# Where the second modulation is applied, and where the first expert's weights lie

## What is computed

```python
def trunk_layer(x, mods, p, ctx_kv_c, ctx_k_rope):
    shift1, scale1, gate1, shift2, scale2, gate2 = mods
    mix, c_kv, k_rope = token_mixer(x * (1 + scale1) + shift1, p, ctx_kv_c, ctx_k_rope)
    x = layer_norm(ALPHA * x + gate1 * mix, p['ln1_g'], p['ln1_b'])
    ffn = expert_choice_ffn(x * (1 + scale2) + shift2, p)
    x = layer_norm(ALPHA * x + gate2 * ffn, p['ln2_g'], p['ln2_b'])
    return x, c_kv, k_rope

def expert_choice_ffn(h, p):
    ...
    aff = jax.nn.softmax((tok @ p['w_router']).astype(jnp.float32), axis=-1)
    gate, idx = lax.top_k(aff.T, cap)
    xe = tok[idx]
    hid = jax.nn.silu(jnp.einsum('ecd,edf->ecf', xe, p['w_gate'])) * jnp.einsum('ecd,edf->ecf', xe, p['w_up'])
    ye = jnp.einsum('ecf,efd->ecd', hid, p['w_down']) * gate[..., None].astype(tok.dtype)
    ...
```

## Time and profile before

| What | Value |
|---|---|
| Time of three executions | 2191.76 us median (2188.12 to 2195.24) |
| Profiled execution | 2196.62 us, span 2194.8 us |
| PE busy | 2067.1 us, 94% of the span |
| DVE, ACT, POOL busy | 985.7, 181.4, 103.2 us |
| Read from memory | 649.44 MB, mean 299 GB/s |
| Mean granted TensorE clock | 0.981 |
| Chain that ended last | PE 73%, DMA 18%, DVE 6% |
| Expert gate and up matmuls (L1228) | 2048, 469.9 us busy, 43.6 us idle before them, of it 30.6 for w_gate loads |

### The profile page before, as it was taken

One profiled execution on the slowest core, in us unless ns is written; L12 is line 12 of the kernel. 1 busy time (PEld: TensorE's weight loads), 2 busy tenths in 40 slices (PEclk: granted clock), 3 DMA queues, 4 the chain that ended last, 5 costly groups with the idle time before them and its releaser, 6 DMA issues.

```text
span 2194.8 us, 21927 instructions
## 1 busy us (share of the span) xinstructions
PE 2067.1 (94%) x9470; PEld 1217.4 (55%) x9470; DVE 985.7 (45%) x1289; ACT 181.4 (8%) x418; POOL 103.2 (5%) x156
## 2 busy tenths in 40 slices
PE   6999999999999999999998999999999999989886
PEld 3455455555799999998874533333333333322222
DVE  4221365729799898997565221121112212121114
ACT  2111310000011111111010000000000000000000
POOL 1010010002110000100000000000000000000001
PEclk8999999999999999999999899999999999999998
DMA  9993036603376666667669699999999999999992
GB/s 344 402 347 115 0 114 218 229 20 106 113 242 233 220 231 232 228 230 282 238 245 368 247 405 435 431 430 430 430 432 431 432 429 426 431 433 430 430 429 115
DMA packets 138426, 657.39 MB, mean 300 GB/s; under 512 B 7137, under 2 KB 83643, under 8 KB 114201
## 3 DMA queue, kind: packets, MB, share of 16 engines
q1 hardware_dynamic: 125538, 586.05, 66.8%
q0 software_dynamic: 12304, 69.86, 8.8%
q10 hardware_dynamic: 488, 0.08, 0.0%
HBM read 649.44 MB, written 6.52 MB: 299 GB/s over the span
## 4 chain that ended last, share of the span: by engine, by line
PE 73%; DMA 18%; DVE 6%; SPq 1%; issue 1%; ACT 0%; DVEq 0%; ACTq 0%
DMA ring<-in_w_up_dram 13%; PE ps L1228 12%; PE ps L927 12%; PE ps L1262 8%; PE ps L1428 8%; PE ps L933 6%; PE ps L993 4%; DMA ring<-in_w_gate_dram 4%; PE ps L864 2%; PE ps L1045 2%; PE ps L736 2%; PE ps L1153 1%; PE ps L701 1%; PE ps L748 1%; PE ps L1170 1%; PE ps L1154 1%
## 5 line engine op out<-in xcount | busy, mean ns | idle before, releaser
L1228 PE MATMUL ps<-ring,arena 128*64 128x512 f32 (+1 forms) x2048 | 469.9, 604 | 43.6 <-DMA ring<-in_w_gate_dram 30.6
L1228 PEld LDWEIGHTS ps<-ring,arena 128*64 128x64 f32 (+1 forms) x2048 | 145.2, 138 | 355.6 <-issue 289.2
L2440 DVE TENSOR_TENSOR arena<-ps,arena 128x512 f32<-128x512 f32 x180 | 116.0, 686 | 398.5 <-PE ps L1170 398.5
L1262 PE MATMUL ps<-ring,arena 128*64 128x512 f32 x1024 | 224.6, 594 | 6.9 <-DMA ring<-in_w_down_dram 5.6
L1784 DVE SCALAR_TENSOR_TENSOR arena<-ring,arena 128x2048 f32<-128x2048 f32 x90 | 211.4, 2349 | 2.1
L927 PE MATMUL ps<-arena,ring 128*128 128x192 f32 x1024 | 174.4, 326 | 0.1
L927 PEld LDWEIGHTS ps<-arena,ring 128*128 128x128 f32 x1024 | 167.6, 190 | 1.5 <-issue 1.2
L1428 PE MATMUL ps<-arena,ring 128*128 128x384 f32 x512 | 165.6, 486 | 0.0
L1262 PEld LDWEIGHTS ps<-ring,arena 128*64 128x64 f32 x1024 | 71.5, 137 | 147.8 <-issue 135.9
L1428 PEld LDWEIGHTS ps<-arena,ring 128*128 128x128 f32 x512 | 97.2, 190 | 68.2 <-issue 0.9
L927 PE MATMUL ps<-ring 128*128 128x192 f32 x768 | 132.7, 326 | 0.0
(11 more groups left out here) (361 smaller groups left out, 1819.3 us busy)
## 6 DMA issues: line engine op xcount, KB each, us to landing
ring<-in_w_gate_dram SPq DMA_DIRECT2D x30, 4096.0 KB, 20.4
ring<-in_w_up_dram SPq DMA_DIRECT2D x30, 4096.0 KB, 21.8
ring<-in_w_down_dram SPq DMA_DIRECT2D x28, 4096.0 KB, 20.7
ring<-in_w_in_dram SPq DMA_DIRECT2D x29, 2048.0 KB, 8.6
ring<-in_w_ada_dram POOLq DMA_DIRECT2D x48, 1024.0 KB, 5.2
ring<-in_w_ada_dram SPq DMA_DIRECT2D x32, 1024.0 KB, 18.0
ring<-in_w_out_dram SPq DMA_DIRECT2D x16, 2048.0 KB, 11.5
ring<-in_w_ada_dram SPq DMA_DIRECT2D x8, 2048.0 KB, 12.9
```

The source lines that it names most:

```text
L1228: mm = pe.matmul(ps[j // 4][64 * half:64 * half + m, :], xe_w[g % 2][:, c0:c0 + m], w[:, k4, half * 512:(half + 1) * 512], start=(k == 0), ...
L1262: mm = pe.matmul(ps[3 + u % 2][64 * half:64 * half + 64, :], hidT[:, k % 4, 64 * (k // 4):64 * (k // 4) + 64], w[:, k2, u * 512:(u + 1) * ...
L2440: dve.tensor_tensor(out, ps[SCATTER_BANKS[q % 5]][:, :], out, ALU.add).then_inc(S["cb_used"], 1)
```

## The change

- h2 holds only the normalised rows: `modulated` becomes `normalised`, one instruction per half instead of two. Scale and shift are applied where D lies on the partitions: in the copies of the transposed tiles (for the router) and in the copies of the gathered rows (for the experts), with one number per partition (`col_r`, `col_e`) as pointer operands. Each copy of 512 or 384 columns becomes four instructions, one per block and, for the gathered rows, per group of tokens.
- The spread rows `mod_s` and `mod_c` go. POOL loads `col_e` and `mod_blocks` in eight small loads instead; PE transposes `mod_blocks` once, in latent unit 1, and DVE copies it to `col_r`.
- Blocks 6 and 7 of expert 0 (the last two up blocks) get memory of their own, `early`, in Y + 4096 and A_HT, and are issued ahead of all other expert blocks. The later blocks' places move up by two: (n - 2) % 6. The two regions of xe change places, and give and ye move.
- ln1 is loaded when PE has released block 6, and all three residuals stand together in expert 0, ahead of ye.
- Three semaphores of the front are merged into one (`ld_front`); these hunks are left out below, as are the lists of names.

```diff
@@ -78,9 +78,10 @@
     N_X0 = stream.index(("x0", 0, 0))
+    EARLY = (N_EXP + 6, N_EXP + 7)
...
                 (n - N_GATE) % 2 * 2 if n < N_OUT else OUT_PLACES[n - N_OUT] if n < N_EXP else
-                (n - N_EXP) % RING for n in range(N_ALL)]
+                n - N_EXP if n < EARLY[0] else None if n in EARLY else (n - N_EXP - 2) % RING for n in range(N_ALL)]
@@ -115,7 +116,6 @@
         x1T = view(A_MG + 3072, 2, NT)
-        mod_c = view(A_HT, 2, D)
@@ -131,6 +131,9 @@
         tri = view(o + 256, P)
+        col_r = view(o + 128, 2, 2, KD)
+        col_e = view(o + 192, 2, 2, KD)
+        mod_blocks = view(o + 418, P, parts=64)
@@ -249,7 +252,6 @@
         gate1 = view(Y, 2, D)
-        mod_s = view(Y + 4096, 2, D)
@@ -260,11 +262,12 @@
         XE = KD * GRP * 48
-        xe_off = (A_HT, Y)
+        early = [view(Y + 4096, SLOT), view(A_HT, SLOT)]
+        xe_off = (Y, A_HT)
...
         xe_w = [view(off, XE) for off in xe_off]
-        give = view(A_HT + XE, 3, GRP, P)
-        ye = view(A_HT + XE + 1536, 2, 512)
+        give = view(A_HT + 4096, 3, GRP, P)
+        ye = view(A_HT + XE, 2, 512)
...
@@ -313,11 +316,13 @@
         for n in range(N_ALL):
+            if n in EARLY:
+                continue
...
         def slot(n, *dims):
-            ap = ring[:, place_of[n], 0:math.prod(dims)]
+            ap = early[n - EARLY[0]] if n in EARLY else ring[:, place_of[n], 0:math.prod(dims)]
@@ -377,7 +382,10 @@
-            eng.wait_ge(used[place_of[n]], turn_of[n] + 1)
+            if n in EARLY:
+                eng.wait_ge(S["early_used"], n - EARLY[0] + 1)
+            else:
+                eng.wait_ge(used[place_of[n]], turn_of[n] + 1)
...
@@ -479,9 +487,16 @@
+            sp.wait_ge(S["ada_rows"], 6)
+            sp.dma_start(slot(EARLY[0], 4, FF), w_up_v[:, 0, 8:12, :]).then_inc(ld_early, 16)
+            sp.wait_ge(S["wo_done"], 16)
+            sp.dma_start(slot(EARLY[1], 4, FF), w_up_v[:, 0, 12:KD, :]).then_inc(ld_early, 16)
+
...
                     n = N_EXP + 12 * e + j
+                    if n in EARLY:
+                        continue
@@ -646,21 +661,21 @@
             pool.dma_start(w_router[:, :, 0:NE], t["w_router"][0].rearrange("(k p) n -> p k n", p=P)).then_inc(ld_wr, 16)
-            pool.wait_ge(S["wo_done"], 3)
-            for j in range(2):
-                pool.dma_start(mod_s[:, j, :], row(mods_dram[1 + j, 1], P)).then_inc(ld_mods, 16)
+            for kind in range(2):
+                for j in range(2):
+                    r0 = 32 * kind + 16 * j
+                    pool.dma_start(mod_blocks[r0:r0 + 16], mods_dram[1 + j, kind].rearrange("(k p) -> k p", p=P))\
+                        .then_inc(ld_mods, 16)
+                    pool.dma_start(col_e[:, kind, j, :], mods_dram[1 + j, kind].rearrange("(p k) -> p k", k=KD))\
+                        .then_inc(ld_mods, 16)
...
             pool.dma_start(gate1[:, 0, :], row(mods_dram[0, 0], P)).then_inc(ld_x2b, 16)
-            pool.wait_ge(S["wo_done"], 16)
-            for j in range(2):
-                pool.dma_start(mod_c[:, j, :], row(mods_dram[1 + j, 0], P)).then_inc(ld_modc, 16)
-            pool.wait_ge(S["h2_done"], 4)
+            pool.wait_ge(S["route_ps"], 5)
+            pool.memset(give.rearrange("p a b c -> p (a b c)"), 0.0).then_inc(gp, 1)
+            through(pool, EARLY[0])
...
             pool.dma_start(ln1[:, 1, :], row(t["ln1_b"][0], P)).then_inc(ld_ln1, 16)
-
-            pool.wait_ge(S["route_ps"], 5)
-            pool.memset(give.rearrange("p a b c -> p (a b c)"), 0.0).then_inc(gp, 1)
@@ -684,10 +699,13 @@
                     n -= (n - N_EXP) % 2
-                pe.wait_ge(full[place_of[n]], filled[n])
+                if n in EARLY:
+                    pe.wait_ge(ld_early, 32)
+                else:
+                    pe.wait_ge(full[place_of[n]], filled[n])
...
             def release(mm, n):
-                mm.then_inc(used[place_of[n]], 1)
+                mm.then_inc(S["early_used"] if n in EARLY else used[place_of[n]], 1)
@@ -1008,6 +1026,9 @@
                 out_product(r1, rows_11, w_11, True).then_inc(S["prod_ps"], 1)
+                if cb == 1:
+                    pe.wait_ge(ld_mods, 128)
+                    pe.transpose(ps[6][:, 0:64], mod_blocks, ident[0:64, 0:64]).then_inc(S["col_ps"], 1)
...
@@ -1665,8 +1686,12 @@
                         act.wait_ge(S["route_ps"], 2 * p - 1)
-                    act.activation(h2T[:, 4 * q:4 * q + 4, :].rearrange("p a b -> p (a b)"), ps[2 + q][:, :], ACT.Copy)\
-                       .then_inc(S["h2T_a"], 1)
+                    for b in range(4):
+                        kb = 4 * q + b
+                        ins = act.activation(h2T[:, kb, :], ps[2 + q][:, b * P:(b + 1) * P], ACT.Identity,
+                                             bias=col_r[:, min(TILES[p], 1), 0, kb:kb + 1],
+                                             scale=col_r[:, min(TILES[p], 1), 1, kb:kb + 1])
+                    ins.then_inc(S["h2T_a"], 1)
@@ -1684,6 +1709,7 @@
             table(ACT.Exp)
+            act.wait_ge(S["col_done"], 3)
@@ -1697,16 +1723,23 @@
                 act.wait_ge(S["xe_ps"], 8 * g + i + 1)
-                act.activation(xe[g % 2][:, 2 * i:2 * i + 2, :].rearrange("p a b -> p (a b)"), ps[bank][:, 0:384],
-                               ACT.Copy).then_inc(S["xe_a"], 1)
-
-            act.wait_ge(S["h2_done"], 6)
+                for k in (2 * i, 2 * i + 1):
+                    src = ps[bank][:, k % 2 * 192:k % 2 * 192 + 192].rearrange("p (a b) -> p a b", b=48)
+                    dst = xe[g % 2][:, k, :].rearrange("p (a b) -> p a b", b=48)
+                    for kind, cs in ((1, slice(0, CAP_S)), (0, slice(CAP_S, 48))):
+                        ins = act.activation(dst[:, :, cs], src[:, :, cs], ACT.Identity, bias=col_e[:, kind, 0, k:k + 1],
+                                             scale=col_e[:, kind, 1, k:k + 1])
+                ins.then_inc(S["xe_a"], 1)
+
+            act.wait_ge(ld_mods, 128)
+            act.wait_ge(S["wo_done"], 20)
...
                                          ps[half][:, kk * 128:(kk + 1) * 128].rearrange("p (a b) -> p a b", b=CAP_S),
-                                         ACT.Copy)
+                                         ACT.Identity, bias=col_e[:, 1, 0, 4 * half + kk:4 * half + kk + 1],
+                                         scale=col_e[:, 1, 1, 4 * half + kk:4 * half + kk + 1])
@@ -2279,17 +2312,13 @@
-            def modulated(p):
+            def normalised(p):
...
                 tile = TILES[p]
-                mods, ready = (mod_c, ld_modc) if tile == 0 else (mod_s, ld_mods)
-                dve.wait_ge(ready, 32)
...
                     cs = slice(half * 1024, (half + 1) * 1024)
-                    link(dve.scalar_tensor_tensor(h2[:, tile, cs], acc[:, tile, cs], lnv[:, tile, 0:1], mods[:, 1, cs],
-                                                  ALU.subtract, ALU.mult))
-                    dve.scalar_tensor_tensor(h2[:, tile, cs], h2[:, tile, cs], lnv[:, tile, 3:4], mods[:, 0, cs],
-                                             ALU.mult, ALU.add).then_inc(S["h2_done"], 1)
+                    dve.tensor_scalar(h2[:, tile, cs], acc[:, tile, cs], lnv[:, tile, 0:1], lnv[:, tile, 3:4],
+                                      ALU.subtract, ALU.mult).then_inc(S["h2_done"], 1)
@@ -2311,8 +2340,12 @@
                         dve.wait_ge(S["route_ps"], 2 * p - 1)
-                    dve.tensor_copy(h2T[:, 4 * q:4 * q + 4, :].rearrange("p a b -> p (a b)"), ps[2 + q][:, :])\
-                       .then_inc(S["h2T_d"], 1)
+                    for b in range(4):
+                        kb = 4 * q + b
+                        ins = dve.tensor_scalar(h2T[:, kb, :], ps[2 + q][:, b * P:(b + 1) * P],
+                                                col_r[:, min(TILES[p], 1), 1, kb:kb + 1],
+                                                col_r[:, min(TILES[p], 1), 0, kb:kb + 1], ALU.mult, ALU.add)
+                    ins.then_inc(S["h2T_d"], 1)
@@ -2370,31 +2403,33 @@
                     out_mix(cb + 1, 3)
+                if cb == 1:
+                    dve.wait_ge(S["col_ps"], 3)
+                    link(dve.tensor_copy(col_r.rearrange("p c m k -> p (c m k)"), ps[6][:, 0:64]))
+                    dve.sem_inc(S["col_done"], 1)
             spread(1, 1)
-            modulated(0)
+            normalised(0)
...
             h2T_copies(0)
-            modulated(1)
+            normalised(1)
...
             context_rows(1)
-            residual(0)
...
             context_rows(2)
-            residual(1)
...
             spread(0, 3)
-            modulated(2)
+            normalised(2)
@@ -2429,8 +2464,13 @@
                 dve.wait_ge(S["xe_ps"], 8 * g + i + 1)
-                dve.tensor_copy(xe[g % 2][:, 2 * i:2 * i + 2, :].rearrange("p a b -> p (a b)"), ps[bank][:, 0:384])\
-                   .then_inc(S["xe_d"], 1)
+                for k in (2 * i, 2 * i + 1):
```

(27 more changed lines are left out.)

12 lines of the change are left out of this document (6 added, 6 removed).

## The result

The changed kernel takes **2209.63 us** in the median of five executions (2205.86 to 2215.91); the kernel before takes 2191.76 (2188.12 to 2195.24) beside it. The ratio is 1.0082, 95% interval 1.0068 to 1.0096: slower by 15 to 21 us, more than the 0.3% that a measurement can tell. I had forecast 2189.0, no change, with a range of 2180 to 2201.

What follows compares the result with a forecast made beforehand. A PE-bound front, then a DMA-bound back started by blocks 14, 15: -6.6 us up to there, +1.2 for g2 and +2.6 for PE's late restart, -2.8 in sum, so 2189.0 us on the median, range 2180 to 2201.

Steps and rivals of the forecast that it cites:

- The bound: PE-bound front, DMA-bound back; everything after 1272.8 us hangs on when the pair of blocks 14, 15 is issued.
- signs that I had named for being wrong: Block 14 issued much earlier than PE's gain, DMA share 1.00 from 1250, or first-scatter wait zero or above 15 us.
- The two early slots: Expert 0's up blocks 6, 7 loaded early; costed at nothing, since the same release still frees blocks 14, 15.
- Residuals out of the routing: Second softmax without the residual on DVE ahead of it: PE's stop of 2.83 us and 1.7 us of low clock go, -4.5 us.
- Normalise only, third tile: Third tile before the router: shorter normalising on DVE, PE transposes sooner, router products end earlier, -3.3 us.
- Copies of the gathered rows: One ACT copy of 384 before PE's next weights becomes four pieces: +1.0 us, bounds +0.4 and +1.4.
- One transpose more: Second latent unit on PE: one extra transpose, +0.2 us; its wait for small loads taken as 0, bounds 0 and +1.8.
- the third rival: Faster: small return in expert 0 and the low clock of 1202 to 1224 spared (1.7 us), total -7.1, 2184.7 us; chance 0.20.
- what comes back in expert 0: Late residuals, g2 and ye delay PE's first scatter of expert 1 by 7.7 us; +2.6 after slack, +1.2 for g2.
- g2's landing: Expert 0: POOL's four g2 loads, issued after the residuals, the last landing 6.3 us later.
- The slower rival: Expert 0: ln1 starves beside the weight queue (28.5 us), ye waits: 2206 us, slower from ye 15.4 us late; chance 0.16.
- The slack: At the issue of block 26: PE may be 5.1 us late for free, including 2.35 us of start-up.

Runs made afterwards that it cites:

- e9: Changed kernel, early slots kept, residuals in DVE's gaps as in e4, ln1 not loaded and bias-row scaling left out (timing only): 2188.63 us, ratio 0.9976.
- e11: The kernel of e4 again, run beside e9 and e10: 2187.96 us, ratio 0.9983 to the kernel before.
- e10: Kernel before, with only the first residual moved behind the second softmax and the second one place later: 2188.46 us, ratio 0.998.
- e2: Changed kernel, with expert 1's weight blocks issued one by one instead of in pairs: 2200.92 us, ratio 1.0033 to the kernel before.
- e1: Changed kernel, with the four g2 loads issued by SyncE on the weights' queue ahead of block 18: 2198.41 us, ratio 1.0026 to the kernel before.
- e5: e4 with one wait more: POOL issues g2's loads only when PE has released block 11 of expert 0: 2202.17 us, ratio 1.0044 to the kernel before.
- e8: The changed kernel again, unaltered, beside e5 to e7: 2208.91 us, ratio 1.0074 to the kernel before.
- e6: e4 with all three residuals moved to DVE's idle time before expert 0's first product: 2188.7 us, ratio 0.9981 to the kernel before.
- e7: e4 with the first residual back ahead of the second softmax: 2192.28 us, ratio 1.000 to the kernel before.
- e4: Changed kernel without early slots, ln1 loaded early behind gate1, the three residuals in DVE's gaps: 2186.17 us, ratio 0.9965 to the kernel before.
- e3: Changed kernel with the two early slots undone, the rest kept: 2212.61 us, ratio 1.0084 to the kernel before.

## Why the prediction was wrong

**The bound held.** Everything behind 1260.4 hung on one queue, and what PE lost beyond the slack came out at the end. Of the signs that I had named for being wrong, one came: the wait at the first scatter above 15 us.

**The two early slots** are worth nothing, as costed: e9 against e11. The hole moved as said: in the changed kernel the DMA share is 0.00 from 1257 until 14, 15 are issued at 1260.4, not at the 1266 that I named. That is 3.4 us of dry engines, where I had named over 5. From the start of PE's first half group for the prompt (at 1128.0, in the changed kernel at 1123.2) to that issue the kernel before takes 144.8 us, the changed one 137.2. That is -7.6, and with +0.9 for the transpose ahead of it **-6.7, where the sum had -6.6**. By its terms:

- *Residuals out of the routing*: taken -4.5, measured -4.7 (59.4 us against 54.7 from that start to the group at 1187.35, in the changed kernel at 1177.90). e10 has -3.6 for the whole kernel.
- *Normalise only, third tile*: taken -3.3, measured -3.4 (32.4 against 29.0 to the first gate matmul). The eight copies on ACT took 0.36 us each, for the 0.40 I took.
- *Copies of the gathered rows*: taken +1.0, measured +0.9. Four pieces took 1.40 us where one of 384 took 0.49. The estimate from the Trainium skill (VectorE: DVE Perf Modes, the section on the TRN2 errata) was +0.43; the trace has the same sign and twice the size, and the measurement decides.
- *One transpose more*: taken +0.2 with a wait of 0. The wait was 0.64, within the bounds of 0 and 1.8.
- *The clock behind the routing*, which only the third rival had: the first 16 gate matmuls took 4.87 us at a granted clock of 0.74 (1206.9 to 1211.7), before 5.34 us at 0.67 (1219.7 to 1225.1). That gave 0.5 us, not the rival's 1.7.

So the sum agrees to 0.1 us partly because small misses cancel: 0.7 us more for the transpose, 0.5 less by the clock, 0.4 less in the other terms.

**The step that failed is "what comes back in expert 0", in the term of g2's landing: 6.3 us taken, 20.2 measured.** (6.3 is the median of the four loads; the last of them took 6.8 in the kernel before.) ln1 landed at 1257.7. In the frame of before (12.4 us later) that is 1270.1, 3 us past the 1267 that I took. The residuals took 15.8 us for 15.5. POOL's issue took 1.8 for 2.3. Then I had 6.3, from the earlier trace rows, and PE's stop became 22.92 + 2.2 = 25.2 us, where I had 7.7. Of the 17.5 us between, 13.9 are g2's landing and about 3 are ln1's.

The row was right and read in the wrong place. These are the DMA queues of the kernel before in 1240 to 1249, while it loads g2 (q1 is the weights' queue, q0 is POOL's: packets, MB, share):

```profile
q1 hardware_dynamic: 181, 2.70, 77.5%
q0 software_dynamic: 192, 0.52, 22.9%
```

And of the changed kernel in 1275 to 1296:

```profile
q1 hardware_dynamic: 240, 6.82, 85.7%
q0 software_dynamic: 192, 0.52, 6.9%
```

g2 is the same 192 packets and 0.52 MB. Before, it passed 181 weight packets of 15 KB each; after, 240 packets of 28 KB each. In number the two queues go roughly in step, in bytes the small one waits for 6.82 MB and not for 2.70. The Trainium skill (DMA: Bandwidth & Descriptors, Queues, rings and completion order) says that the engines take turns between queues packet by packet; these two rows agree with it. That a small load lands late beside large packets is what I drew from it, and stands on the rows, not on the page. I had used that very rule for ln1 and not for g2, although my own working moved g2's issue from 1240, beside single blocks, into the stretch of 1275 to 1342, where blocks are loaded in pairs. I even charged the saturated stage with g2's bytes (+1.2 us) and left its latency as it was.

Busy engines are not what differs. By the rows above they were full at the old place too (77.5% and 22.9%). The same holds for ln1, whose quick landing I had put down to w_out being nearly alone: from 1144 to 1154 in the kernel before the DMA share was 0.95, but the weights' queue moved 1.48 MB in 721 packets, 2 KB each. Beside ln2, which took 28.5 us, its packets had 29 KB (40.63 MB in 1392).

Nor do packets in step give the whole of it. In e2, in 1276 to 1290, the weight packets had 14 KB, as at the old place:

```profile
q1 hardware_dynamic: 314, 4.41, 88.6%
q0 software_dynamic: 192, 0.52, 11.9%
```

Yet 314 of them passed beside g2's 192, where 181 did before, and the last load took 13.16 us where it took 6.8. Halving the packets took a third off the landing, not half. What else sets it no run isolates.

**The slower rival had the right mechanism, the wrong load and too high a threshold.** It let ln1 starve; ln1 landed in 14.1 us. It said that the kernel is slower, by over 6.6 us, from 15.4 us of lateness of ye on; ye was 22.9 late. But with stops of 12.3, 14.1 and 14.3 us e1, e2 and e5 are already 6.1, 8.6 and 9.6 us slower than the kernel before. Its chance of 0.16 was too low because I asked only of the first load in the row what it meets, and not of the second.

**The slack** was 4.0 us up to the landing of blocks 26, 27. I had taken 5.1, but with 1.2 us for g2's bytes both in it and charged beside it, so 3.9 net. With the parts as measured in the profiled pair the sum is -6.7 + 25.2 - 4.0 + 1.7 = +16.2. The 1.7 is not worked out on its own: it is what the end shows beyond that landing (10.5 - 8.8), and no run isolates it. By the medians of the changed kernel, e1, e2 and e8, with the stop and the slow matmuls behind it from their traces, what the DMA absorbed in the end is only 0.6 to 2.3 us. That fits the lower threshold.

e1, e2 and e5 each vary one thing about g2's load and move PE's stop and the total together; e6 and e9 clear the residuals' place on DVE and the slots. That g2's lateness is the cause is shown. That e7 and e10 together make e4 and e11 fits the terms (0 and -3.6 against -4 to -6), but one gap isn't settled: e7's median is 4 to 6 us above those of e4 and e11, and the stop explains 2.7 us of it (from the group of 16 ahead of it to the third tile's transposes there are 35.2 us in e7, 32.5 in e4). A low clock may be the rest. The one behind this stop, seen in the kernel before, is not in e7's profiled execution, but there is another behind the copies of the gathered rows:

```profile
1238.04 19.08 PE L1231 MATMUL ps<-ring,arena 128*64 128x512 f32 x80 [1.54 <-issue]
```

In e4 and e11 the same 80 matmuls behind the same 1.54 us take 17.39. e3 and e9 lost the same 1.7 us here. The split copies made this stop longer (0.63 us in the kernel before and in e10, with no loss behind it), so they may have a price that the +0.9 leaves out. It fell in three of the eleven profiled executions that have the longer stop; no run isolates it.

## What to carry to other kernels

A load's landing time belongs to the place where it was read: when a step moves, price every load in its chain again, by the size of the packets in the queue that it will share, not by its own bytes and not by how busy the engines are. Small loads that a chain waits for go out before the large packets begin, or on the stream's own queue, which here took 10.0 us for 20.2. And where DVE has gaps, moving the work there may give all that the larger change was after: here two moved lines gave 3.6 us, while the change that freed the same place cost 18, and the modulation per partition with the residuals in the gaps (e4, e11) gave 4 to 6.

## What was not expected of the hardware

The last of four loads of 128 KB landed after 5.9 us in e4 and 6.8 in the kernel before, 13.2 beside single-block weight loads (e2), 17.7 to 20.2 beside paired ones (e5, the changed kernel, e8), 10.0 beside a weights' queue that was running out (e3), and 10.0 in line on the weights' queue (e1). In the changed kernel the four took 9.5 to 20.2 us though they were issued within 1.5 us: the later ones waited behind the first.

The granted clock after a stop isn't a fixed price. After 2.96 us of idle time 16 matmuls of 256 columns took 6.61 us in one execution, at a granted clock of 0.55, and after 2.94 us 3.69 in another, at 1.00; 2.83 us were followed by 15.60 us for 32 matmuls of 512 columns, 2.48 us by 13.90. After stops of 12.3 to 25.6 us the first four scatters took 2.08 us each time, where 1.13 is usual, and the 16 matmuls behind them took 4.38 to 5.75 us, where 3.65 is usual. Short stops may or may not cost the clock, and 1.7 us for one is a value between 0 and 2.9.
